# Moving tile 1's group products between the expert layers to the two places around tile 0's turn

## What is computed

```python
def mixer_pool(h, w_in, w_grp, scale, w_out):
    m = multiscale_pool(h @ w_in)                       # sums over windows of 2, 4, 8, 16 tokens
    m = jnp.einsum('btgc,gce->btge', m.reshape(bsz, t, 4, 256), w_grp)
    return (m.reshape(bsz, t, 1024) * scale) @ w_out
...
xs = layer_norm(alpha * xs + g1 * yx, ln_g[i, 0], ln_b[i, 0])
hx = modulate(xs, sh2, sc2)
fx = peer(hx, peer_wq[i], peer_keys[i], peer_u[i], peer_v[i])
```

## Time and profile before

| | |
|---|---|
| median of 3 runs | 2109.28 us |
| lowest, highest | 2108.14, 2113.47 us |
| the profiled execution's own time | 2111.44 us |
| its span in the trace | 2109.5 us |
| PE busy in the span | 1788.1 us (85%) |
| DVE busy | 1460.5 us (69%) |
| ACT busy | 915.6 us (43%) |
| POOL busy | 620.7 us (29%) |
| DMA, mean over the span | 342 GB/s |
| mean granted TensorE clock | 0.969 |

### The profile page before, as it was taken

One profiled execution on the slowest core, in us unless ns is written; L12 is line 12 of the kernel. 1 busy time (PEld: TensorE's weight loads), 2 busy tenths in 40 slices (PEclk: granted clock), 3 DMA queues, 4 the chain that ended last, 5 costly groups with the idle time before them and its releaser, 6 DMA issues.

```text
span 2109.5 us, 22456 instructions
## 1 busy us (share of the span) xinstructions
PE 1788.1 (85%) x7309; PEld 1074.2 (51%) x7309; DVE 1460.5 (69%) x3032; ACT 915.6 (43%) x2391; POOL 620.7 (29%) x573
## 2 busy tenths in 40 slices
PE   4887999899988799997877787988999977877776
PEld 3756998788877454443232232454654422322222
DVE  6676867777776677766767677527677667677675
ACT  2446433534473344444444444324444444444443
POOL 1170000000001344543344333213455443443431
PEclk9889999999998999999999999999999999999999
DMA  9753668555565899999999999957999999999996
GB/s 368 284 200 119 251 230 312 202 207 205 195 220 205 329 422 420 421 421 418 420 421 422 422 421 421 369 204 298 394 417 421 421 422 422 421 422 421 421 422 257
DMA packets 114269, 721.72 MB, mean 342 GB/s; under 512 B 11460, under 2 KB 13300, under 8 KB 33640
## 3 DMA queue, kind: packets, MB, share of 16 engines
q0 software_dynamic: 74864, 540.30, 61.9%
q1 hardware_dynamic: 39288, 179.99, 23.4%
HBM read 719.16 MB, written 1.08 MB: 341 GB/s over the span
## 4 chain that ended last, share of the span: by engine, by line
DMA 36%; PE 33%; DVE 15%; ACT 7%; issue 5%; POOL 3%; SPq 0%; DVEq 0%; ACTq 0%; POOLq 0%
DMA X<-in_k_uv,EI 24%; DMA Z<-in_k_uv,EI 11%; PE PS L2274 10%; PE PS L1952 4%; PE PS L1954 4%; PE PS L1953 4%; DVE junk L1939 4%; PE PS L2250 3%; DVE ACC L1560 2%; POOL X L1070 2%; DVE WL L1576 2%; PE PS L2047 2%; DMA W<-in_ada_w 1%; ACT WH L1079 1%; PE PS L2291 1%
## 5 line engine op out<-in xcount | busy, mean ns | idle before, releaser
L2274 PE MATMUL PS<-X,dg 128*128 128x512 f32 x1380 | 665.1, 614 | 131.0 <-ACT dg L1079 130.3
L1939 DVE CUSTOM_DVE_ANT_0 junk<-H,X 128x1024 f32<-128x1024 f32 x345 | 422.0, 1223 | 242.3 <-DMA X<-in_k_uv,EI 237.4
L1070 POOL DMA_INDIRECT X<-in_k_uv,EI x345 | 369.8, 1072 | 510.9 <-PE PS L2274 325.1
L2274 PEld LDWEIGHTS PS<-X,dg 128*128 128x128 f32 x1380 | 248.3, 193 | 506.0 <-ACT dg L1079 292.9
L1079 ACT ACTIVATE CF<-DOT 128x1 f32<-128x1 f32 x512 | 103.6, 202 | 655.7 <-DVE DOT L1939 654.9
L2274 PE MATMUL PS<-Z,dg 128*128 128x512 f32 x480 | 235.5, 618 | 56.7 <-ACT dg L1079 56.4
L1079 ACT ACTIVATE dg<-CP,CG 128x128 f32<-128x128 f32 x512 | 205.5, 401 | 19.1 <-PE PS L2274 2.5
L1939 DVE CUSTOM_DVE_ANT_0 junk<-H,Z 128x1024 f32<-128x1024 f32 x120 | 146.8, 1223 | 92.6 <-DMA Z<-in_k_uv,EI 90.2
L2274 PEld LDWEIGHTS PS<-Z,dg 128*128 128x128 f32 x480 | 84.9, 191 | 188.2 <-ACT dg L1079 119.3
L1952 PE MATMUL PS<-XH,WH 128*128 128x256 f32 x592 | 174.9, 296 | 2.7 <-ACT XH L1079 1.2
L1953 PE MATMUL PS<-XL,WH 128*128 128x256 f32 x592 | 170.2, 287 | 0.0
(11 more groups left out here) (322 smaller groups left out, 2600.5 us busy)
## 6 DMA issues: line engine op xcount, KB each, us to landing
W<-in_ada_w SPq DMA_DIRECT2D x56, 1024.0 KB, 5.8
Y<-in_ada_w SPq DMA_DIRECT2D x16, 1024.0 KB, 6.0
W<-in_k_win SPq DMA_DIRECT2D x16, 1024.0 KB, 5.0
W<-in_k_ffi SPq DMA_DIRECT2D x13, 1024.0 KB, 6.4
Y<-in_k_ffi SPq DMA_DIRECT2D x9, 1024.0 KB, 4.9
W<-in_ffn_w_out SPq DMA_DIRECT2D x8, 1024.0 KB, 5.7
W<-in_peer_wq SPq DMA_DIRECT2D x8, 1024.0 KB, 13.4
W<-in_ab_w_out SPq DMA_DIRECT2D x6, 1024.0 KB, 5.0
```

Source lines behind the costliest of these rows:

```text
L1070: e.indirect_dma_start(out=WS[k][:, :], out_offset=None, in_=I[f"k_uv{ly}"][:, :], in_offset=bass.IndirectOffsetOnAxis(ap=EI[t][:, j:j + 1 ...
L1939: e.tensor_tensor_reduce(junk, H[:, t, :], d[:, 0:D], 1.0, 0.0, ALU.mult, ALU.add, DOT[:, j:j + 1]).then_inc(v_dot, 1)
L2274: p = e.matmul(PS[:, 2 * t + q, :], dgb[n % 4][:, :], d[:, D + q * 512:D + (q + 1) * 512], start=(j == 0), stop=(j == 127))
```

## The change

For tile 1 of layer 1 the group products leave their place between the scores of head 1 and the output product. Four chunks go in front of tile 0's turn, into bank 6 (128 columns each); four go behind its transposes, into bank 7. Their copies by ACT become a step of their own, `grpe`: four behind ACT's part of the turn, two behind the copy of query chunk 0, two behind that of query chunk 1. A copy waits until all four chunks of its bank are there. `take` is called once for each bank. Tile 0's group products (`grp` 0) are as they were. `po` of tile 1, which writes banks 6 and 7, now waits in `take` for the copies out of them.

```diff
--- before.py
+++ after.py
@@ ramp @@
         if ly == 0:
             P("modp", 9, 2)
+        if ly:
+            for c in range(4):
+                P("grp", 1, c, 6)
         P("tt", ly, 0)
+        if ly:
+            for c in range(4, 8):
+                P("grp", 1, c, 7)
+            for c in range(4):
+                P("grpe", c)
         if ly == 0:
             P("mod", 9, 2)
         for i in range(2):
             plan.extend(narrow(ly, 0, 0, i, 4 + i))
+            for c in range(4 + 2 * i, 6 + 2 * i):
+                if ly:
+                    P("grpe", c)
         P("rt", ly, 0, 0, 0)
@@ ramp @@
         else:
-            for c in range(8):
-                P("grp", 1, c, c % 2)
             P("po", 1)
             plan.extend(pieces[2:])
@@ ACT @@
-                elif kind == "grp":
-                    t, c, b = a
-                    w.wait_ge(p_grp, nth("grp", t, c))
-                    act(chunk(m2, c, t), PS[:, b, 0:128], ACT.Copy, scale=C2[:, c_psc + c:c_psc + c + 1]).then_inc(
+                elif kind == "grp" and a[0] == 0 or kind == "grpe":
+                    t, c, b = a if kind == "grp" else (1, a[0], 6 + a[0] // 4)
+                    o = c % 4 * 128 if t else 0
+                    w.wait_ge(p_grp, nth("grp", t, c | 3 if t else c))
+                    act(chunk(m2, c, t), PS[:, b, o:o + 128], ACT.Copy, scale=C2[:, c_psc + c:c_psc + c + 1]).then_inc(
                         a_grp, 1)
@@ PE @@
-                    take(b)
+                    o = c % 4 * 128 if t else 0
+                    if o == 0:
+                        take(b)
                     for k in range(2):
-                        p = e.matmul(PS[:, b, 0:128], wg[:, g, k, (c % 2) * 128:(c % 2) * 128 + 128],
+                        p = e.matmul(PS[:, b, o:o + 128], wg[:, g, k, (c % 2) * 128:(c % 2) * 128 + 128],
                                      chunk(mT, 2 * g + k, t), start=(k == 0), stop=(k == 1))
```

## The result

| | before | changed | same change, measured a second time |
|---|---|---|---|
| median, us | 2109.22 (13 runs) | 2103.68 (13 runs) | 2103.22, against 2108.43 for the kernel before |
| ratio to before, 95% interval | | 0.9982 [0.9973, 0.999] | 0.998 [0.9971, 0.9989] |
| profiled execution, us | 2111.44 | 2105.04 | |
| its span / granted clock | 2109.5 / 0.969 | 2103.0 / 0.966 | |

The ratio of 0.9982 is 3.8 us less, with an interval of 5.7 to 2.1 us; the second measurement gives 4.2 us. The sum forecast 3.9. The two medians lie 5.5 and 5.2 us apart, more than the ratios say, but inside both intervals (the second is 6.1 to 2.3 us); this text goes by the ratios.

The account below looks back on a forecast made before the run. The prediction took the stream of 256 gathers to set the end, with the change only starting or filling it earlier. Its terms, 0.25 - 2.5 - 1.67 = -3.9 us from 2109.28, gave 2105.4 us, range 2101.9 to 2110.3.

Parts of the forecast that it names:

- The sum: DVE, PE and gather chain to the end: +0.25 - 2.5 - 1.67 = -3.9 us at the median.
- What bounds the kernel: Layer 1's expert layer: the stream of 256 gathers sets the end; the change can only start or fill it earlier.
- Products in the waits: PE around tile 0's turn: sixteen records of 1.87 us per wait; first costs nothing, second delays the queries +0.25 us.
- The clock: PE's first query block: clock stays at 2.4 GHz, 3.74 us for 6.69, -2.95 us; counted 2.5 at the median.
- ACT's copies: DVE's reciprocal: copies hidden in ACT's idle time, so the exponential no longer delays it, -1.67 us.
- `po` earlier: PE's tile 1 output product: reached 4.4 us earlier from the move alone, 7.1 in all; counted 0.
- Carried through to the seventeenth gather: DVE's gain, -4.37 us in the profile, passes through PE's tails to the seventeenth gather and the end, 4.4 us earlier.
- The list of what to see: Trace signs: short query block, no reciprocal wait, first gather near 1432.6, third to sixth gathers not waiting for PE L2342.
- The second slow stretch: Rival, PE behind tile 1's turn: the clock's fall goes there too, 3.1 us more gained, 2102.3 us; chance 0.13.
- The clock falls all the same: Rival, first query block: clock falls anyway, or did not fall in the median's executions; -1.4 us, 2107.9 us; chance 0.22.
- Hidden gain: Rival, gather stream: queued gathers hold the pace and earlier DVE only waits longer; about 2109.3 us; chance 0.1.
- Slower through the waits between the tails: Rival, PE between `po` and sixth tail: 2.7 us more waiting lowers the clock; at worst 2110.8 us; chance 0.07.

Follow-up runs that it names:

- filling both waits alone: Kernel before plus sixteen idle products, or idle transposes, around tile 0's turn, group products left in place: 0.9994 (-1.3 us) and 0.9991 (-1.9 us).
- the kernel with the wait put back: Changed kernel plus seventeen idle ACT copies ahead of the exponential's table load, so the reciprocal waits for ACT again: 0.9993, -1.5 us.
- `po` at 22.26: Changed kernel plus 20 idle products before tile 1's output product: 0.9981, -4.0 us.
- at 26.73: Changed kernel plus 40 idle products before tile 1's output product: 0.9999, -0.2 us.
- `po` left at 25.16 us: Kernel before with pieces 2 to 5 of head 0's search put ahead of tile 1's group products, waits unfilled: 1.0008, +1.7 us.
- at 23.65: Kernel before with idle products in both waits and the exponential ahead, group products left in place: 0.999, -2.1 us.
- one wait filled: Changed kernel with only chunks 0 to 3 moved; chunks 4 to 7 and their copies back just before `po`, on bank 7: 0.9983, -3.6 us.

## Why the prediction was right, step by step

**What bounds the kernel** held. The windows of the changed kernel in pieces of 32 us from the band's start (busy PE, PEld, DVE, ACT, POOL, clock, DMA share, GB/s):

```profile
1408.03:1440.03 32.00, 30.82 (x178) 22.25 (x177) 23.80 (x77) 11.04 (x33) 5.83 (x6) 1.00 0.28 99
1440.03:1472.03 32.00, 22.35 (x73) 11.24 (x74) 24.38 (x49) 17.20 (x46) 13.10 (x12) 0.95 1.01 422
```

The same pieces of the kernel before:

```profile
1409.38:1441.38 32.00, 27.68 (x162) 22.51 (x161) 19.84 (x63) 10.86 (x29) 3.90 (x3) 0.89 0.22 78
1441.38:1473.38 32.00, 25.07 (x74) 11.89 (x73) 26.26 (x61) 17.56 (x47) 14.53 (x13) 0.97 0.99 400
```

The first piece gains 21 GB/s and a clock of 1.00, the second 22 GB/s. The stream starts and fills earlier; its pace stays 422 GB/s.

**Products in the waits, +0.25 us.** Right in kind; the queries start 0.11 us later (8.49 us behind the band's start, 8.38 before). The sixteen records take 1.95 us and not 1.87, and leave 0.25 us before the turn and nothing behind it.

**The clock, -2.95 us in the profile, 2.5 at the median.** Right for the profile (6.69 to 3.74). The guess for the median is the weak step: filling both waits alone gave 1.3 and 1.9 us, together 1.6 (0.6 to 2.7), net of the later start, where 2.25 was counted. That unfilled executions don't all lose the whole 2.95 fits with the block of 5.36 us under the same waits; how often it is long, short or between is open, since each unfilled kernel has one profile only. The interval includes 2.25.

**ACT's copies, -1.67 us.** Right at the reciprocal, which is 1.70 us sooner beyond what the clock gives, and in the sign of the time. Its size is not settled. The tails carry only some 1.0 us of it, because the first two dots now wait for their gathers, while the times give it 2.2 us, or 2.7 by the kernel with the wait put back. By the times the clock's term came out smaller than counted and this one larger, some 1.6 + 2.2 against 2.25 + 1.67; by the profiles it is the other way round, 2.85 + 1.0. Either way the two misses offset each other, and that the sum of 3.9 came out so close is in part luck.

**`po` earlier, counted at 0.** The text asked whether `po`'s earlier start is worth anything by itself, and answered no because nothing on the path asks for it. That reason was incomplete. `po` releases the tiles of the third to sixth gathers, and once DVE is 4.4 us early these are near the path: with `po` at 22.26 us nothing is lost, at 26.73 3.8 us are. Before, `po` started at 25.04, between the two. With `po` left at 25.16 us an early reciprocal gained nothing (1.0008), which speaks for `po` having to move forward for the gain to be paid; by how much isn't shown. The change moves it far enough, so the 0 held, but the text didn't see the condition.

**Carried through to the seventeenth gather.** Only -3.81 of the -4.54 us reach the tails. The missing 0.7 goes at the first two dots, which now wait 0.34 and 0.22 us for their gathers and come 4.12 and 3.81 us sooner. DVE got ahead of the stream's start, which the text did not foresee: EI and the first gather are 2.86 us earlier, the reciprocal 4.54. At the seventeenth gather, which waits for the ninth tail to end, it is -4.12, because that tail's four records took 3.46 us and not 3.78. The list of what to see had one line not quite right: the third to fifth gathers no longer wait for PE L2342, but the sixth still does, 1.87 us, where it waited 2.50.

**The second slow stretch** (rival, 0.13) came in part. From the start of the ninth tail to the end of the two query groups behind it, it is 6.5 us before and 5.1 after, and this is about the difference between -3.81 at the ninth tail and -5.08 at the end. No run ties it to the change: with the 3.40 us of waiting behind tile 1's turn left open, the four records took 3.78 us in two other kernels (`po` at 22.26 and at 23.65), 3.16 to 3.68 in six more profiles (the changed kernel's second one among them), and 1.98 in two. The rival's price of 3.1 us fits the 2.9 us between 6.5 and the 3.6 us with one wait filled; its "as much again" for the query products doesn't, they lost 1.1.

**The clock falls all the same** (0.22): not seen in any profile with a filled wait. The rival's other half, that it did not fall in all the executions that make the median, may hold in part, as the clock's term above says, but 1.4 us in all is outside both intervals. **Hidden gain** (0.1): excluded by both intervals. **Slower through the waits between the tails** (0.07): PE does wait 2.02 us there, 2.9 us more in all between the tails than before where 2.7 were reckoned, and the records behind the 2.02 us take 1.98 us at clock 1.00. The Trainium skill's warning of short bursts at half rate (HAM oscillation — how this bites in real kernels, on the same page) is not seen in this stretch; the case that it tells has waits of 3 to 5 us between its bursts.

## What to carry to other kernels

When you make one engine early, look for what else its next steps need. A term that holds in the trace can be worth nothing alone if another wait, here the release of tiles by `po`, comes right behind it. Measure the slack of a step that you count at nothing with idle work in doses; here a delay of 4.5 us cost nothing, and one of 8.9 us cost 3.8. Compare profiles at a point close behind the change, and sizes by the times of several kernels that share it. And price a change of clock at the median with less than its profile shows, unless more than one profile shows it.

## What the runs showed of the hardware

- With fp32 transposes in both waits the granted clock stayed at 2.4 GHz: the first query block took 3.81 us behind 3.2 us of transposes, and 6.69 us where only the turn's own 1.09 us stood there.
- The same unfilled waits, of 2.04 and 1.51 us, gave a block of 6.69 us in one kernel and 5.36 us in another, and four tail records behind the same wait of 3.40 us took 1.98 us in two kernels' profiles and 3.16 to 3.78 us in ten.
- With the turn at 1.09 us and one group of 1.95 us in front of it, a wait of 1.51 us left the clock at 2.4 GHz.
